# Chunk scan of a Mamba-2 layer: the decay exponent split between VectorE and ScalarE

## The reference, cut to what matters

```python
def ssd_chunk(state, xs, dt, a, bm, cm):
    ...
    cum = jnp.cumsum(dt * a, axis=1)
    seg = cum[:, :, None] - cum[:, None, :]
    causal = jnp.tril(jnp.ones((q, q), dtype=bool))[None, :, :, None, None]
    decay = jnp.exp(jnp.where(causal, seg, -jnp.inf))
    cb = jnp.einsum('btgn,bsgn->btsg', cf, bf)
    w = cb[..., None] * decay * dt[:, None]
    y = jnp.einsum('btsge,bsgep->btgep', w, xf)
    y = y + jnp.einsum('btgn,bgepn->btgep', cf, state) * jnp.exp(cum)[..., None]
    ...
```

## Time and profile before

| | |
|---|---|
| median of 3 runs | 3108.25 us |
| the runs | 3109.15, 3108.25, 3097.89 us |
| profiled execution, time | 3096.53 us |
| profiled execution, span | 3094.7 us |
| mean granted TensorE clock in it | 0.929 |
| TensorE matmul busy | 2741.9 us |
| VectorE busy | 1457.8 us |
| ScalarE busy | 770.9 us |
| the scan's nine chunks | about 2063 to 2554 us of the span |

### The profile page before, as it was taken

How to read it: one execution, slowest core, us unless ns; L and a number is a source line. 1 busy time by engine, 2 the same in 40 slices (tenths; PEclk the granted TensorE clock), 3 DMA queues, 4 the chain that set the end, 5 groups by cost and what they waited for, 6 DMA issues and landing times. The chain is left out here.

```text
span 3094.7 us, 40148 instructions
## 1 busy us (share of the span) xinstructions
PE 2741.9 (89%) x16283; PEld 2191.0 (71%) x16283; DVE 1457.8 (47%) x2553; ACT 770.9 (25%) x1452; POOL 520.9 (17%) x419
## 2 busy tenths in 40 slices
PE   5999898998968999998999599758999995899899
PEld 4998566675856997677999377545555534699677
DVE  4998666665311005545565500347767643100453
ACT  3221354332212212322322211121212111121231
POOL 1012000341301210122221000003222211121012
PEclk9999899997989998998999799887999897899999
DMA  3212001861031114203221211493242304111431
GB/s 101 60 35 53 15 35 51 306 240 38 1 123 55 48 61 158 96 1 80 85 94 68 84 72 70 123 313 103 62 121 61 76 1 136 48 48 42 170 115 51
DMA packets 235642, 270.75 MB, mean 87 GB/s; under 512 B 36502, under 2 KB 190678, under 8 KB 230243
## 3 DMA queue, kind: packets, MB, share of 16 engines
q1 hardware_dynamic: 215650, 179.85, 19.2%
q0 software_dynamic: 16384, 75.77, 6.7%
q10 hardware_dynamic: 3456, 12.98, 1.0%
HBM read 226.66 MB, written 41.28 MB: 87 GB/s over the span
## 5 line engine op out<-in xcount | busy, mean ns | idle before, releaser
L297 PE MATMUL pp<-HH,WS_part 128*128 128x352 f32 x1776 | 575.2, 324 | 0.0
L295 PE MATMUL pp<-HH,WH 128*128 128x352 f32 x1344 | 437.5, 325 | 40.1 <-POOL WS_part L434 40.1
L296 PE MATMUL pp<-HT_part,WH 128*128 128x352 f32 x1344 | 435.5, 324 | 0.0
L297 PEld LDWEIGHTS pp<-HH,WS_part 128*128 128x128 f32 x1776 | 337.4, 190 | 0.0
L295 PEld LDWEIGHTS pp<-HH,WH 128*128 128x128 f32 x1344 | 255.2, 190 | 42.1 <-POOL WS_part L434 42.1
L2748 PE MATMUL OP<-oWO,YT 128*128 128x512 f32 (+1 forms) x576 | 252.4, 597 | 4.0 <-DVE XE L2873 3.3
L296 PEld LDWEIGHTS pp<-HT_part,WH 128*128 128x128 f32 x1344 | 255.2, 190 | 0.0
L434 POOL TENSOR_TENSOR WS_part<-WS,WH 128x1024 fp32r<-128x1024 f32 x56 | 143.9, 2570 | 652.8 <-ACT WH L385 652.8
L2211 DVE COPY HT<-zT 128x512 f32<-128x512 f32 x64 | 44.3, 692 | 439.1 <-DMA xown<-c_batch 385.4
L2748 PEld LDWEIGHTS OP<-oWO,YT 128*128 128x128 f32 (+1 forms) x576 | 104.0, 182 | 144.4 <-issue 140.8
L1048 DVE SCALAR_TENSOR_TENSOR CV<-GXP,cw,CV 128x512 f32<-128x512 f32 x240 | 162.0, 746 | 0.0
(11 more groups left out here) (499 smaller groups left out, 5160.6 us busy)
## 6 DMA issues: line engine op xcount, KB each, us to landing
WS<-x_w_qg SPq DMA_DIRECT2D x32, 512.0 KB, 4.1
WO<-cache_mem_k SPq DMA_DIRECT2D x16, 1024.0 KB, 5.0
WO<-cache_mem_v POOLq DMA_DIRECT2D x16, 1024.0 KB, 5.5
CBt<-cum_scratch SPq DMA_DIRECT2D x8, 2048.0 KB, 10.1
xbc_scratch<-oACC ACTq DMA_DIRECT2D x24, 528.0 KB, 2.7
WS<-o_w_in SPq DMA_DIRECT2D x24, 512.0 KB, 3.8
XT<-xbc_scratch SPq DMA_DIRECT2D x8, 1536.0 KB, 7.5
WS<-e_w_in SPq DMA_DIRECT2D x18, 512.0 KB, 3.9
```

What stands on the lines that cost most here:

```text
L295: nc.tensor.matmul(out, wh, xh, start=start, stop=False)
L296: nc.tensor.matmul(out, wh, xl, start=False, stop=False)
L297: return nc.tensor.matmul(out, wl, xh, start=False, stop=stop)
```

## The change

VectorE no longer subtracts the own sum. It takes the smaller of the two sums, `min(cum[t], cum[s])`, with one `tensor_tensor` for each group of 8 heads (four of 128x1024 in place of 32 of 128x128). ScalarE subtracts the own sum as the bias of the exponential, and since the bias is one value for each partition, it needs one instruction for each head: 32 of 128x128 in place of four of 128x1024. A new small tile `ncu` holds the negated own sums, made by one more VectorE instruction in each chunk. The waits and semaphore counts between the engines stay as they were: `r_seg` after each group, `r_ex` after each group's last exponential.

```diff
-            dts, cus = sb(c, "dts", [P, SH]), sb(c, "cus", [P, SH])
+            dts, cus, ncu = (sb(c, n, [P, SH]) for n in ("dts", "cus", "ncu"))
...
                     for g in range(4):
                         act.wait_ge(r_seg, n * 4 + g + 1)
-                        nc.scalar.activation(CB[R, g * HP:(g + 1) * HP, R], CB[R, g * HP:(g + 1) * HP, R], ACT.Exp)\
-                            .then_inc(r_ex, 1)
+                        for h in range(g * HP, (g + 1) * HP):
+                            ins = nc.scalar.activation(CB[R, h, R], CB[R, h, R], ACT.Exp, bias=ncu[R, h:h + 1])
+                        ins.then_inc(r_ex, 1)
...
-                    v(N.tensor_copy(cus[R, :].unsqueeze(1), CUt[R, bass.ds(n, 1), :]))
+                    dve_own.did(N.tensor_copy(cus[R, :].unsqueeze(1), CUt[R, bass.ds(n, 1), :]))
+                    v(N.tensor_scalar(ncu[R, :].unsqueeze(1), CUt[R, bass.ds(n, 1), :], -1.0, None, ALU.mult))
...
                     for g in range(4):
-                        for e in range(HP):
-                            h = g * HP + e
-                            ins = N.tensor_scalar(CB[R, h, R], CB[R, h, R], cus[R, h:h + 1], 0.0, ALU.subtract, ALU.min)
-                        ins.then_inc(r_seg, 1)
+                        part = CB[R, g * HP:(g + 1) * HP, R]
+                        N.tensor_tensor(part, part, cus[R, g * HP:(g + 1) * HP].unsqueeze(2).to_broadcast([T, HP, T]), ALU.min)\
+                            .then_inc(r_seg, 1)
...
-                run(dve, chunk, out, dve_own, 6)
+                run(dve, chunk, out, dve_own, 7)
```

## The result

The changed kernel takes 3114.33 us (median of 9 runs, 3109.08 to 3119.09), the kernel before in the same comparison 3097.89 (9 runs, 3088.14 to 3109.15). The ratio is 1.0048, with a 95% interval of 1.0032 to 1.0064: the change costs about 15 us, where 24 us of gain were forecast. The profiled execution took 3115.59 us (span 3113.8), 19 more than that of before.

A forecast was written before the change was run, and what follows sets the result against it. TensorE was taken as the bound, VectorE counting only where TensorE waits. 1.7 us (chunk 0), 3.9 (pauses) and 18.4 (clock) made 24.0, which taken from a median of 3108.25 gave 3084 us, range 3067 to 3109.

The forecast's parts named there:

- VectorE's part: Scan, each chunk: four minima save 1.73 us over 32 subtractions, `ncu` costs 0.1; VectorE reaches L2905 1.63 us earlier.
- the prediction's signs: Trace signs of a right forecast, among them L2905 starting 7.5 us behind the first minimum's start, and L2792 unbroken.
- ScalarE's part: L2845, each chunk: 32 exponentials of 387 ns, 292 ns from start to start, 9.44 us, just in time, nothing lost.
- The step that failed: In ScalarE's part: the claim that no DMA or GpSimd instruction is moved; no time was set against it.
- the forecast's sum: Whole kernel: 1.7 in chunk 0, 3.9 for pauses and 18.4 for the clock, 24.0 us saved.
- What reaches the end: Gain by chunk: 1.7 us in chunk 0, none in 1 and 8, 3.9 for pauses in 2 to 7, clock 18.4.
- the price of lateness: If VectorE came 1.2 us later: 7.4 us lost in chunks 2 to 7, 1.2 in chunk 0, 3.4 from chunk 2's fall.
- the third rival: L2845 on ScalarE: biased exponentials don't overlap, VectorE comes 1.2 us later; 12.5 us slower, 3121 us, chance 0.07.
- The clock: L2792 on TensorE, chunks 2 to 7: without the pause the clock holds as in chunk 1, 18.4 us saved.
- The range: Whole kernel, 3067 to 3109 us: holds the forecast with scatter and the first two rivals, leaves out the third.
- one slower case: The third rival: ScalarE's exponentials become the bound, 12.5 us slower, 3121 us, chance 0.07.
- its base of 3108.25 us: Median of the kernel before, from which 24.0 us were taken to forecast 3084.

The follow-up runs named there:

- e6_later_wide: e1_skip_later with ScalarE's four wide exponentials of the kernel before, own sum left out of the exponent; ratio 0.9916 beside 0.9913 for e1_skip_later.
- e1_skip_later: Changed kernel with GpSimd's skip product waiting for XE (chunk 8: last product) instead of XD; 3068.55 us, ratio 0.9913 to the kernel before.
- e9: Changed kernel plus one small VectorE tensor_scalar (128x128, one SBUF operand) between the minima and the mask product; 3071.21 us, a single run.
- e5_pause: e1_skip_later with TensorE waiting before group 2 for the evictions of both groups 0 and 1; ratio 1.0032, 37 us above e1_skip_later.
- b1_before_later: Kernel before with only GpSimd's skip product moved to wait for XE, nothing of the change; ratio 0.9994.
- e11: Changed kernel with four wide exponentials, own sum left out of the exponent, plus the small extra VectorE instruction of e9; 3067.04 us, ratio 0.9902.
- e10: Changed kernel plus one VectorE tensor_tensor (128x1024, two SBUF operands) between the minima and the mask product; 3075.04 us, a single run.
- e7: Changed kernel with VectorE waiting for all exponentials before XD, GpSimd's wait unchanged; 3174.78 us, a single run.
- e12: e7 plus the small extra VectorE instruction of e9, placed in front of that wait; 3176.87 us, a single run.

## Why the prediction was wrong, point by point

- **VectorE's part** was right: minima 4.63 us, `ncu` 0.17, the products begin 7.35 us behind the first minimum instead of 9.07; with `ncu` in front that is the 1.63 us forecast. (The 7.5 us among the prediction's signs doesn't fit its own sum, 2234.40 - 2227.06 = 7.34.)
- **ScalarE's part** was right: 387 ns each, 0.292 from start to start, 9.46 us, and it costs nothing (e6_later_wide).
- **The step that failed** is one sentence: "No DMA and no GpSimd instruction is moved." L2728 starts with XD's end, so the change moved it, and it stood beside the products the whole time. The prediction took the products at 1.14 us each from rows in which VectorE shut GpSimd out, and did not ask why a GpSimd instruction took 10.14 us there. The Trainium skill had it: the page "SBUF — State Buffer", section "Who interferes with whom", says that a VectorE instruction with two SBUF inputs contends with a GpSimd instruction that reads SBUF. The same page of the Trainium skill, section "Summary: rules for kernel authors", says that of two such instructions the one issued second stands still until the first is done, and advises arranging them by which is off the critical path. The traces agree on the standing still (4.64 us for a 1.22 us product; 10.14 for a 3.62 us one), but in the kernel before they don't bear out the order: GpSimd's record starts 0.97 us ahead of the second product's, and GpSimd waits. This one term is the distance between forecast and result: in e1_skip_later, where GpSimd is out of the way, the scan is 24.0 us shorter in the trace, the forecast's sum (27 us by the measured ratio). That the sum is met to the tenth is luck: chunk 0 gave 1.0 us where 1.7 were forecast, and chunks 2 to 7 gave 23.0 where 22.3 were. In e9, where GpSimd keeps its place and loses as in the kernel before, the single run lies 23.5 us under that kernel's median.
- **What reaches the end**: the price of lateness was right in kind. With VectorE 1.8 us later at the pause than in the kernel before, the pauses are 1.8 us longer, where the third rival had 1.2 and blamed ScalarE. That rival's shape (longer pauses, a fall in chunk 2 too, longer falls in four of the other five chunks) is what happened, with GpSimd in ScalarE's place.
- **The clock** was right, on one chunk's evidence: without a pause it holds (e1_skip_later, chunks 1 to 7), with one put back it falls (e5_pause, six of seven). Of the two sections of the Trainium skill's page "TensorE: Matmul & The Clock Gate" weighed in the prediction, the second ("A second HAM failure mode"), on short idle spells between groups, is the one that these runs bear out.
- **The range** reached 3109 and left out a loss, since its one slower case hung on the pace of ScalarE alone; the second engine on VectorE's operands was in none of the cases. Two of its numbers were off besides: its base of 3108.25 us lay 10.4 above the 3097.89 that nine runs gave, and its lower end takes 27 us off the fastest run where its own sum is 24.0. Neither decided the outcome.

## What to carry to other kernels

When a VectorE instruction is timed from a trace, look at what GpSimd has running beside it: a GpSimd instruction nearly three times as long as it is elsewhere was here a wait, and the engine that won before the edit lost after it. Order the two by a semaphore that puts the GpSimd work behind the critical products, as e1_skip_later does: the changed kernel is 15 us slower than the kernel before without it and 27 us faster with it. By itself the semaphore is worth nothing (b1_before_later). And in this kernel a pause of 0.63 to 0.71 us among short matmuls was followed in five chunks of six by a fall of the clock that cost 3.3 to 5.0 us.

## What the runs showed of the hardware

The winner is not simply the one that starts first. In the kernel before GpSimd's record starts 0.97 us ahead of VectorE's second product and still waits through three products and XE; in the changed kernel, from the same distance, it wins. With one VectorE instruction more in front of the mask product (0.22 us in e9 and e11, 1.22 in e10) GpSimd stayed out of the second product in every chunk of 128 in the three kernels. In e7 and e12, where VectorE had stood idle for 5.4 to 7.6 us in front of XD, GpSimd won in 18 chunks of 18. No run here tells why.

A blocked instruction showed no idle time here. It is counted as busy, so the waits view and the idle column have nothing on it; only its length, against the same form elsewhere, gives it away.
